# GLA mixer of a hybrid layer: 64-row TensorE tiles in place of zero padding, one output bank per head parity, and a later projection placed inside the pair loop

## The chip, the cores and the metric

One NeuronCore of a Trainium2 chip runs one program of two layers. The metric is the device time of one execution in microseconds (us). PE is TensorE, DVE VectorE, ACT ScalarE, POOL GpSimd, SP the queue that issues the weight loads. All arithmetic is fp32; a matmul in fp32 shows as two passes in the trace, so 16 records are 8 matmuls (a transpose is one pass).

## The reference

Two post-norm layers over 128 context tokens and 256 latent tokens. Each layer has three token mixers (gated DeltaNet, GLA, differential attention), a merge, an output projection and a grouped top-2 mixture of 16 experts. The change is in GLA and in the query projection of the attention that follows it. GLA, per head (4 heads, 64 key by 128 value dims, chunks of 64 tokens, forward and backward):

```
b = cumsum(glog)                    # within a chunk
a_intra = where(incl, (q*exp(b-b_ref)) @ (k*exp(b_ref-b)).T, 0)
q_dec, k_tail, g_tail = q*exp(b), k*exp(b_last-b), exp(b_last)
def step(S, xs):                    # over the chunks
    o = q_dec @ S + a_intra @ v
    S = S * g_tail[:, None] + k_tail.T @ v
```

The output is `o_forward + flip(o_backward)`, RMS-normed per head, times SiLU of a gate, and goes with the two other branches into the merge.

## The kernel before

One instruction stream is written out by hand for each engine; nothing is scheduled by a planner. The 384 tokens are three tiles of 128 (tile 0 the context, tiles 1 and 2 the latent grid). PSUM is used as seven banks in rotation: `take` on PE waits until the bank's last reader has freed it, `full` and `drained` are the waits of the other side. Weights come through a ring of three 2 MB slots, loaded by SP in the order in which PE's code first asks for them (`arrived`); a slot is loaded again when the product that used it has ended.

After DeltaNet a layer runs the dense products `gqk`, `gv`, `r` (24 matmuls of 128x512 each, line 395), then the GLA pair loop, then the product `dq` (the query projection of the attention), `finish_branch` for GLA, and the products `dk` and `dv`.

The pair loop (`PAIRS`, line 644) runs over three pairs p of (forward tile, backward tile): (0,0), (1,2), (2,1). In each pair:
- L650 and L657 form the decay sums on PE; ACT takes their exponentials (L1348 to L1355), DVE multiplies q and k into them (L1720), PE transposes the products (L666), ACT copies them out of PSUM (L1360, L1363, L1365).
- L675 makes the intra-chunk scores. Two heads share 128 key rows; so that a head sees only its own 64, the query operand `gl_qz` is kept twice, with the other head's half zero, and every matmul contracts over 128 rows. DVE masks the scores (L1726), one bank per direction d.
- L682 multiplies them with v; DVE moves the result into the output `ov` (L1734, L1730).
- Two steps, one per chunk. In each, for d = 0 and then d = 1, L702 multiplies the carried state into a bank of its own (DVE adds it to `ov`, L1742) and L712 forms the state's increment, which DVE adds to the decayed state (L1754, four instructions of 64x128). The state has the two heads of a pair side by side, 512 columns with zeros in the halves that belong to the other head.

When the three pairs are done, PE runs two short pieces for a modulation row (L442, L431), then `dq`, and only then waits for `branch_normed` and transposes the normed branch (L421). DVE reaches `branch_normed` after `finish` (L1532 to L1542). The lines of the loop around the wait:

```
                mod_columns(l, 10)
                mod_rows(l, 11)
                slot = arrived(pe, ("dq", l, 0))
                tokens_product("dq", l, lambda k: ring_in[slot][:, k, :])
                chunk_end["dq", l, 0] = ("dq", l, T - 1)
                finish_branch(l, 1)
```

Of the kernel before, what the change touches and what calls it, by code (L numbers as in the profile page):

```python
# [108 lines left out]
def program(nc, a, consts, y_prompt, y_sample, new_gdn, new_gla, new_k, new_v):  # L109
# [5 lines left out]
    with ExitStack() as ctx:  # L115
# [77 lines left out]
        dqv = late[:, 0:T * W5].rearrange("p (t w) -> p t w", t=T)  # L193
# [88 lines left out]
        def gl(name):  # L282

            return u_gla[:, GL[name] * W5:(GL[name] + 1) * W5]

        gl_qz, gl_k, gl_dec = u_gla[:, 3584:4608], u_gla[:, 4608:5120], u_gla[:, 5120:5632]
        gl_ln = u_gla[:, 5632:6144]

        def gla_at(d):
            return tail[:, d * W5:(d + 1) * W5]  # L290

        def gla_state(p, d):
            at = (min(p, 1) * DIR + d) * W5
            return s_gla[:, at:at + W5]
# [86 lines left out]
        def _(pe):  # L381
# [97 lines left out]
            for l in range(DEPTH):  # L479
# [163 lines left out]
                chunk_end["r", l, 0] = ("r", l, T - 1)  # L643
                for p, tiles in enumerate(PAIRS):
# [14 lines left out]
                    mm.then_inc(ready, 1)  # L659
                    for i, name in enumerate(("q_in", "k_in", "q_dec")):  # L660
# [7 lines left out]
                    for d, t in enumerate(tiles):  # L668
                        ps, ready = take(pe, ("gla_a", l, p, d))
                        if d == 0:  # L670
                            drained(pe, ("q_in", l, p))
                            drained(pe, ("k_in", l, p))
                        for h in range(H):
                            hp, par_ = h // 2, h % 2
                            mm = pe.matmul(ps[:, h * P:(h + 1) * P], gl_k[:, (d * 2 + hp) * P:(d * 2 + hp + 1) * P], gl_qz[:, par_ * W5 + (d * 2 + hp) * P:par_ * W5 + (d * 2 + hp + 1) * P],  # L675
                                           start=True, stop=True)
                        mm.then_inc(ready, 1)
                    for d, t in enumerate(tiles):
                        ps, ready = take(pe, ("gla_av", l, p, d))
                        drained(pe, ("gla_a", l, p, d))  # L680
                        for h in range(H):
                            mm = pe.matmul(ps[:, h * P:(h + 1) * P], gla_at(d)[:, h * P:(h + 1) * P],  # L682
                                           gvv[:, t, h * P:(h + 1) * P], start=True, stop=True)
                        mm.then_inc(ready, 1)
                    for step in range(2):
                        for d, t in enumerate(tiles):
                            ch = step if d == 0 else 1 - step
                            tok = slice(ch * HALF, (ch + 1) * HALF)
                            ps, ready = take(pe, ("gla_inter", l, p, d, step))
                            if step == 0 and d == 0:  # L690
                                drained(pe, ("q_dec", l, p))
                            if step == 1:
                                drained(pe, ("gla_ds", l, p, d, 0))
                            elif p == 1 and d == 0:
                                pe.wait_ge(sem("gla_state_in"), 64 * (l + 1))
                            elif p == 2:
                                drained(pe, ("gla_ds", l, 1, d, 1))
                            elif d == 0:
                                pe.wait_ge(sem("gla_zeroed"), l + 1)
                            for hp in range(2):  # L700
                                at = (d * 2 + hp) * P
                                mm = pe.matmul(ps[tok, hp * 256:(hp + 1) * 256], gl_dec[:, at + ch * HALF:at + (ch + 1) * HALF],  # L702
                                               gla_state(p, d)[:, hp * 256:(hp + 1) * 256], start=True, stop=True)
                            mm.then_inc(ready, 1)
                            if p == 2 and step == 1:
                                continue
                            ps, ready = take(pe, ("gla_ds", l, p, d, step))
                            if step == 0 and d == 0:
                                pe.wait_ge(sem("gla_decayed"), (l * 3 + p) * 4 + 4)
                            for hp in range(2):  # L710
                                at = (d * 2 + hp) * P
                                mm = pe.matmul(ps[:, hp * 256:(hp + 1) * 256], gl("k_tail")[tok, at:at + P],  # L712
                                               gvv[tok, t, hp * 256:(hp + 1) * 256], start=True, stop=True)
                            mm.then_inc(ready, 1)
# [339 lines left out]
        def _(pool):  # L1054
# [36 lines left out]
            for l in range(DEPTH):  # L1091
# [72 lines left out]
                for d in range(DIR):  # L1164
                    for hh in range(2):
                        if l:
                            full(pool, ("gla_inter", l - 1, 2, d, 1))
# [879 lines left out]
```

## Time and profile before

| what | value |
|---|---|
| median of 3 runs | 2439.39 us (2436.06 to 2440.36) |
| the profiled execution, first to last instruction | 2440.0 us |
| PE busy in it | 2189.8 us, 90% |
| DVE, ACT, POOL busy | 806.6, 448.7, 214.7 us |
| mean granted clock of PE | 0.966 of full speed |
| stretch from the first decay sum of GLA to the start of `dk`, layer 0 and layer 1 | 83.2 and 81.9 us |

The profiled execution's span is the only time that the page gives for it. A "busy" PE is one with a matmul in flight; a row of the timeline merges neighbouring instructions of one line, gives the start, the length to the end of the last one, their count, and in brackets the idle time before them with what ended it.

### The profile page before, as it was taken

How to read it: one execution, taken by the hardware profiler on the slowest of the kernel's cores; microseconds unless marked ns; L12 is line 12 of the kernel's file. 1: busy time of each engine (PE TensorE's matmuls, PEld its weight loads, DVE VectorE, ACT ScalarE, POOL GpSimd, SP SyncE). 2: the span in 40 equal slices, each digit the busy share in tenths (PEclk: the TensorE clock that was granted, in tenths of full speed). 3: DMA queues.
4: the chain of work that ended last, by engine and by line, in shares of the span. 5: the costliest groups of instructions: out<-in, count | busy, mean ns of one | idle time of the engine just before them, and what ended most of it. 6: DMA issues, size and time to landing. Idle time of an engine off the chain costs nothing.

```text
span 2440.0 us, 25315 instructions
## 1 busy us (share of the span) xinstructions
PE 2189.8 (90%) x9696; PEld 1211.5 (50%) x9696; DVE 806.6 (33%) x1602; ACT 448.7 (18%) x857; POOL 214.7 (9%) x221
## 2 busy tenths in 40 slices
PE   4998899998999879999699889999899978999994
PEld 1557774544444444344355777454444454344342
DVE  0526651625011421111552665162501250111115
ACT  0232114123100211011123111412300121111011
POOL 3024430000000000000002443000000000000000
PEclk9999999999999989999898999999999989999997
DMA  9321113144332359999722121313123228999993
GB/s 326 133 92 59 57 57 104 48 143 159 127 97 99 109 202 349 348 350 350 259 69 102 50 63 51 103 48 112 48 79 100 102 87 319 330 350 369 349 350 127
DMA packets 197474, 407.08 MB, mean 167 GB/s; under 512 B 6178, under 2 KB 6498, under 8 KB 197264
## 3 DMA queue, kind: packets, MB, share of 16 engines
q1 hardware_dynamic: 193136, 393.65, 45.9%
q0 software_dynamic: 4256, 12.28, 1.7%
q8 instruction: 57, 0.93, 0.2%
q14 instruction: 25, 0.20, 0.0%
HBM read 401.72 MB, written 4.19 MB: 166 GB/s over the span
## 4 chain that ended last, share of the span: by engine, by line
PE 72%; DMA 11%; DVE 10%; ACT 3%; issue 2%; SPq 1%; POOL 1%; DVEq 0%; POOLq 0%; ACTq 0%
PE bank L395 24%; DMA ring<-in_exp_w_up 10%; PE bank L545 6%; PE bank L885 6%; PE bank L913 6%; PE bank L873 5%; PE bank L497 5%; PE bank L805 5%; PE bank L923 2%; PE bank L431 1%; PE bank L581 1%; DMA ring<-in_w_mod 1%; PE bank L702 1%; PE bank L712 1%; PE bank L758 1%
## 5 line engine op out<-in xcount | busy, mean ns | idle before, releaser
L395 PE MATMUL bank<-ring,xt 128*128 128x512 f32 x1440 | 623.3, 593 | 8.5 <-ACT shared L1328 2.8
L395 PEld LDWEIGHTS bank<-ring,xt 128*128 128x128 f32 x1440 | 272.2, 190 | 354.2 <-issue 351.8
L885 PE MATMUL bank<-ring,shared 128*64 128x512 f32 x1280 | 295.5, 605 | 54.1 <-DMA ring<-in_exp_w_gate 29.9
L885 PEld LDWEIGHTS bank<-ring,shared 128*64 128x64 f32 x1280 | 88.1, 138 | 254.9 <-issue 167.6
L545 PE MATMUL bank<-shared 128*128 128x128 f32 x1408 | 184.2, 287 | 13.5 <-DVE shared L1678 5.5
L545 PEld LDWEIGHTS bank<-shared 128*128 128x128 f32 x1408 | 176.2, 201 | 15.8 <-issue 15.6
L1929 DVE TENSOR_TENSOR shared<-shared,bank 128x512 f32<-128x512 f32 x20 | 13.8, 688 | 444.6 <-PE bank L885 444.6
L913 PE MATMUL bank<-ring,shared 128*64 128x512 f32 x640 | 141.7, 595 | 1.2 <-issue 1.2
L873 PEld LDWEIGHTS bank<-qkvp,shared 128*128 128x128 f32 x1056 | 124.6, 198 | 20.2 <-issue 17.9
L873 PE MATMUL bank<-qkvp,shared 128*128 128x128 f32 x1056 | 128.8, 284 | 3.8 <-DVE qkvp L1916 3.8
L497 PE MATMUL bank<-xt,ring 128*128 128x384 f32 x384 | 124.3, 486 | 2.8 <-DVE xt L1525 2.8
L805 PE MATMUL bank<-ring,qkvp 128*128 128x512 f32 x288 | 124.7, 592 | 0.0
L1155 POOL TENSOR_TENSOR shared<-shared,cst 128x512 f32<-128x512 f32 x84 | 108.7, 1298 | 128.2 <-DVE shared L1631 63.6
L923 PE MATMUL bank<-shared 128*128 128x512 f32 x240 | 111.3, 601 | 1.5 <-ACT shared L1463 1.5
L497 PEld LDWEIGHTS bank<-xt,ring 128*128 128x128 f32 x384 | 72.8, 190 | 53.5 <-DVE xt L1525 3.2
L1936 DVE TENSOR_TENSOR shared<-shared,bank 128x512 f32<-128x512 f32 x108 | 70.9, 685 | 84.6 <-PE bank L923 84.6
L1446 ACT ACTIVATE shared<-bank 128x512 f32<-128x512 f32 x44 | 26.3, 597 | 344.7 <-PE bank L873 344.7
L805 PEld LDWEIGHTS bank<-ring,qkvp 128*128 128x128 f32 x288 | 54.6, 190 | 68.4 <-issue 68.4
L1833 DVE TENSOR_TENSOR shared<-shared,bank 128x512 f32<-128x512 f32 x24 | 16.5, 688 | 214.7 <-PE bank L805 214.7
L913 PEld LDWEIGHTS bank<-ring,shared 128*64 128x64 f32 x640 | 44.3, 137 | 84.5 <-issue 84.5
L431 PE MATMUL bank<-ring,scol 128*32 128x512 f32 x384 | 57.9, 729 | 26.8 <-DMA ring<-in_w_mod 24.9
L1424 ACT ACTIVATE shared<-bank 128x512 f32<-128x512 f32 x36 | 21.1, 597 | 271.7 <-PE bank L395 271.7
(342 smaller groups left out, 2119.1 us busy)
## 6 DMA issues: line engine op xcount, KB each, us to landing
ring<-in_exp_w_gate SPq DMA_DIRECT2D x80, 1024.0 KB, 7.9
ring<-in_exp_w_up SPq DMA_DIRECT2D x80, 1024.0 KB, 9.8
ring<-in_exp_w_down SPq DMA_DIRECT2D x80, 1024.0 KB, 10.7
ring<-in_w_in SPq DMA_DIRECT2D x32, 2048.0 KB, 9.5
ring<-in_w_mod SPq DMA_DIRECT2D x24, 2048.0 KB, 8.0
ring<-in_w_branch SPq DMA_DIRECT2D x6, 2048.0 KB, 7.7
ring<-in_w_out SPq DMA_DIRECT2D x4, 2048.0 KB, 7.7
shared<-in_ln_g POOLq DMA_DIRECT2D x4, 512.0 KB, 3.8
```

Source lines behind the costliest of these rows:

```text
L395: mm = pe.matmul(ps[:, 0:width], xtv[:, k, t * P:(t + 1) * P], w_of(k), start=(k == 0), stop=(k == KC - 1))
L431: mm = pe.matmul(ps[part:part + 32, :], scv[:, k, :], ring_in[slot][:, k, :], start=(k < 4), stop=(k >= 4))
L497: mm = pe.matmul(ps[:, 0:TOK], ring_in[slot][:, k, m % 4 * P:(m % 4 + 1) * P], xtv[:, k, :], start=(k == 0), stop=(k == KC - 1))
L545: mm = pe.matmul(ps[:, h * P:(h + 1) * P], lhs(h), rhs(h), start=True, stop=True)
L805: mm = pe.matmul(ps[:, :], ot[:, s * 4 + h, t * P:(t + 1) * P], ring_dn[slot][:, h, half * W5:(half + 1) * W5], start=(h == 0), stop=(h == ...
L873: mm = pe.matmul(banks[b][:, k * P:(k + 1) * P], htok[:, t, at:at + P], hot[:, t, :, :].rearrange("p u s -> p (u s)"), start=(t == 0), sto ...
L885: mm = pe.matmul(ps[u * SLOTS:(u + 1) * SLOTS, :], xg[:, at:at + SLOTS], w[:, u, k, :], start=(part == k == 0), stop=(part == 1 and k == 3))
L913: mm = pe.matmul(banks[EXPERT_BANKS["out"][half]][u * SLOTS:(u + 1) * SLOTS, :], ht[:, at:at + SLOTS], w[:, u, m, :], start=(m == 0), stop ...
L923: pe.matmul(banks[EXPERT_BANKS["back"][k]][:, :], hott[:, k // 2 * P:(k // 2 + 1) * P], oe[:, k % 2 * W5:(k % 2 + 1) * W5], start=True, st ...
L1155: pool.tensor_tensor(gd(d, "m").rearrange("p (h i) -> p h i", h=H), gd(d, "lt").rearrange("p (h i) -> p h i", h=H), fan(c(f"level{d}_{v}") ...
L1446: act.activation(xg[:, half * W5:(half + 1) * W5], ps[:, :], ACT.Copy).then_inc(free, 1)
L1936: dve.tensor_tensor(ycut, ycut, ps[:, :], ALU.add).then_inc(free, 1)
```

## The change

The padded operands go. `gl_qz` becomes `gl_q` (one copy, 512 columns), and each GLA state becomes 256 columns without zeros; the memsets of both are dropped. Every matmul on them now contracts over 64 rows and names the rows of its own head (`rows_`), so the two head parities `par_` stand in the upper and the lower 64 rows of the array. The scores of a pair go into two banks by parity, and no longer by direction. Products with v and with the carried state accumulate in the same two banks `gla_o`, which DVE reads once at the end of the pair. The first step of pair 0, whose state is zero, has no carried product, and DVE copies its increment instead of adding it. DVE's state update is two instructions of 128x128 for each step and direction. The product `dq` leaves its place behind the loop: token tile p is computed inside pair p, four matmuls before the transposes and four behind them, and ACT copies it out in the loop. Its result `dqv` moves to another buffer.

```diff
@@ PE, pair loop
+                dq_slot = arrived(pe, ("dq", l, 0))
+                def dq_part(t, part):
+                    if part == 0:
+                        take(pe, ("dq", l, t))
+                    b = fills["dq", l, t][0]
+                    for k in range(part * 4, part * 4 + 4):
+                        mm = pe.matmul(banks[b][:, :], xtv[:, k, t * P:(t + 1) * P], ring_in[dq_slot][:, k, :],
+                                       start=(k == 0), stop=(k == KC - 1))
+                    if part:
+                        mm.then_inc(bank_full[b], 1)
...
+                    dq_part(p, 0)
                     for i, name in enumerate(("q_in", "k_in", "q_dec")):
...
+                    dq_part(p, 1)
+                    pair = [take(pe, ("gla_a", l, p, par_)) for par_ in range(2)]
+                    drained(pe, ("q_in", l, p))
+                    drained(pe, ("k_in", l, p))
+                    for d in range(DIR):
+                        for hp in range(2):
+                            for par_, (ps, ready) in enumerate(pair):
+                                rows_ = slice(par_ * 64, par_ * 64 + 64)
+                                mm = pe.matmul(ps[:, gla_cut(d, hp)], gl_k[rows_, gla_cut(d, hp)], gl_q[rows_, gla_cut(d, hp)],
+                                               start=True, stop=True)
+                                if d == hp == 1:
+                                    mm.then_inc(ready, 1)
+                    out = [take(pe, ("gla_o", l, p, par_)) for par_ in range(2)]
+                    for par_, (ps, _) in enumerate(out):
+                        drained(pe, ("gla_a", l, p, par_))
+                        for d, t in enumerate(tiles):
+                            for hp in range(2):
+                                h = hp * 2 + par_
+                                pe.matmul(ps[:, gla_cut(d, hp)], gla_at(par_)[:, gla_cut(d, hp)], gvv[:, t, h * P:(h + 1) * P],
+                                          start=(d == hp == 0), stop=False, skip_group_check=True)
                     for step in range(2):
+                        if p == 0 and step == 0:
+                            drained(pe, ("q_dec", l, p))
+                        else:
+                            if step == 0:
                                 drained(pe, ("q_dec", l, p))
+                            for d in range(DIR):
+                                if step == 1:
+                                    drained(pe, ("gla_ds", l, p, d, 0))
...
+                            for hp in range(2):
+                                for d in range(DIR):
...
+                                    for par_, (ps, ready) in enumerate(out):
+                                        rows_ = slice(par_ * 64, par_ * 64 + 64)
+                                        mm = pe.matmul(ps[tok, gla_cut(d, hp)], gl_dec[rows_, at:at + HALF],
+                                                       gla_state(p, d)[rows_, hp * P:(hp + 1) * P],
+                                                       start=False, stop=(step == hp == d == 1), skip_group_check=True)
...
+                        pair = [take(pe, ("gla_ds", l, p, d, step)) for d in range(DIR)]
...
+                        for hp in range(2):
+                            for par_ in range(2):
+                                for d, t in enumerate(tiles):
...
+                                    mm = pe.matmul(pair[d][0][par_ * 64:par_ * 64 + 64, hp * P:(hp + 1) * P],
+                                                   gl("k_tail")[tok, at:at + 64], gvv[tok, t, h * P:(h + 1) * P],
+                                                   start=True, stop=True)
+                                    if hp == par_ == 1:
+                                        mm.then_inc(pair[d][1], 1)
...
                 mod_columns(l, 10)
                 mod_rows(l, 11)
-                slot = arrived(pe, ("dq", l, 0))
-                tokens_product("dq", l, lambda k: ring_in[slot][:, k, :])
-                chunk_end["dq", l, 0] = ("dq", l, T - 1)
                 finish_branch(l, 1)
@@ ACT, pair loop
-                    for hh in range(2):
-                        ins = act.activation(gl_qz[hh * 64:hh * 64 + 64, hh * W5:(hh + 1) * W5], ps[hh * 64:hh * 64 + 64, :], ACT.Copy)
-                    ins.then_inc(free, 1)
+                    act.activation(gl_q, ps[:, :], ACT.Copy).then_inc(free, 1)
...
+                    ps, free = full(act, ("dq", l, p))
+                    act.activation(dqv[:, p, :], ps[:, :], ACT.Copy).then_inc(free, 1)
@@ DVE, pair loop, after the masks
+                    for step in range(1 if p == 2 else 2):
...
+                            for hp in range(2):
+                                g0 = (d * 2 + hp) * 2 + ch
+                                ins = dve.scalar_tensor_tensor(out=s[:, hp * P:(hp + 1) * P], in0=s[:, hp * P:(hp + 1) * P],
+                                                               scalar=gla_gt(p)[:, g0:g0 + 1], in1=ps[:, hp * P:(hp + 1) * P],
+                                                               op0=ALU.mult, op1=ALU.add)
                             ins.then_inc(free, 1)
+                    for par_ in range(2):
+                        ps, free = full(dve, ("gla_o", l, p, par_))
...
+                            ins = dve.tensor_copy(o, new) if p == 1 else dve.tensor_tensor(o, o, new, ALU.add)
+                        ins.then_inc(free, 1)
```

Three places in the order of instructions show how this moves work. First PE, pair 1 (the pair in the middle) up to the next decay sum, before; a row counts matmuls and gives the output's partitions and columns:

```order
L657 MATMUL bank<-cst,shared 128x2 x4
L666 MATMUL bank<-cst,shared 128x128 x12
L675 MATMUL bank<-shared 128x128 x8
L682 MATMUL bank<-shared 128x128 x8
L702 MATMUL bank<-s_gla,shared 64x256 x2
L712 MATMUL bank<-shared 128x256 x2
L702 MATMUL bank<-s_gla,shared 64x256 x2
L712 MATMUL bank<-shared 128x256 x2
```

The last two rows come four times in all. The same place now (L660 is `dq_part`, L688 the transposes, L698 the scores, L708 the product with v, L730 the carried product, L746 the increment, L671 the next pair's decay sums):

```order
L678 MATMUL bank<-cst,shared 128x2 x4
L660 MATMUL bank<-ring,xt 128x512 x4
L688 MATMUL bank<-cst,shared 128x128 x12
L660 MATMUL bank<-ring,xt 128x512 x4
L698 MATMUL bank<-shared 128x128 x8
L708 MATMUL bank<-shared 128x128 x8
L730 MATMUL bank<-s_gla,shared 64x128 x8
L746 MATMUL bank<-shared 64x128 x8
L730 MATMUL bank<-s_gla,shared 64x128 x8
L746 MATMUL bank<-shared 64x128 x8
L671 MATMUL bank<-shared,cst 128x256 x6
```

The eight matmuls of `dq` stand around the transposes; both directions' carried products and increments of a step stand together, 8 matmuls of 128 columns where there were 4 of 256. Second, PE at the end of the loop, from the last carried product to `dk`, before:

```order
L702 MATMUL bank<-s_gla,shared 64x256 x4
L442 MATMUL bank<-cst,mrow 128x2 x4
L431 MATMUL bank<-ring,scol 32x512 x8
L395 MATMUL bank<-ring,xt 128x512 x24
L421 MATMUL bank<-cst,otok 128x128 x12
L442 MATMUL bank<-cst,mrow 128x2 x4
L395 MATMUL bank<-ring,xt 128x512 x48
```

And now:

```order
L730 MATMUL bank<-s_gla,shared 64x128 x8
L450 MATMUL bank<-cst,mrow 128x2 x4
L439 MATMUL bank<-ring,scol 32x512 x8
L429 MATMUL bank<-cst,otok 128x128 x12
L450 MATMUL bank<-cst,mrow 128x2 x4
L403 MATMUL bank<-ring,xt 128x512 x48
```

The 24 matmuls of `dq` no longer stand between the end of the loop and the transposes of the normed branch (L429, L421 before). Third, DVE in pair 1, from the masks to the next pair's products, before:

```order
L1726 COPY_PREDICATED shared<-cst,bank 128x512 x2
L1734 COPY otok<-bank 128x512 x2
L1742 TENSOR_TENSOR otok<-otok,bank 64x512
L1754 SCALAR_TENSOR_TENSOR s_gla<-s_gla,small,bank 64x128 x4
L1742 TENSOR_TENSOR otok<-otok,bank 64x512
L1754 SCALAR_TENSOR_TENSOR s_gla<-s_gla,small,bank 64x128 x4
```

The last two rows come four times in all. Now:

```order
L1761 COPY_PREDICATED shared<-cst,bank 128x512 x2
L1778 SCALAR_TENSOR_TENSOR s_gla<-s_gla,small,bank 128x128 x8
L1793 COPY otok<-bank 128x2x128 x4
L1755 TENSOR_TENSOR shared<-shared 128x256 x8
```

The state updates of both steps come first, and the two output banks are read behind the last of them.

## Rows read from the trace of the kernel before

**Rows 1.** The page's head: the span of the profiled execution.
```profile
span 2440.0 us, 25315 instructions
```

**Rows 2.** Timeline of PE in layer 0, GLA to `dk`: start, length, line, count, idle.
```profile
412.40 2.75 PE L650 MATMUL bank<-shared,cst 128*128 128x256 f32 x12
...
420.10 3.00 PE L675 MATMUL bank<-shared 128*128 128x128 f32 x16 [0.20 <-ACT shared L1363]
...
433.33 2.86 PE L650 MATMUL bank<-shared,cst 128*128 128x256 f32 x12
436.03 0.95 PE L657 MATMUL bank<-cst,shared 128*128 128x2 f32 x8
436.84 1.81 PE L666 MATMUL bank<-cst,shared 128*128 128x128 f32 x12
439.46 2.02 PE L675 MATMUL bank<-shared 128*128 128x128 f32 x16 [0.82 <-ACT shared L1363]
441.51 2.02 PE L682 MATMUL bank<-shared 128*128 128x128 f32 x16
443.47 1.08 PE L702 MATMUL bank<-s_gla,shared 128*64 128x256 f32 x4
444.47 1.13 PE L712 MATMUL bank<-shared 64*128 64x256 f32 x4
...
451.73 2.86 PE L650 MATMUL bank<-shared,cst 128*128 128x256 f32 x12
...
457.86 2.02 PE L675 MATMUL bank<-shared 128*128 128x128 f32 x16 [0.82 <-ACT shared L1363]
...
469.25 1.05 PE L442 MATMUL bank<-cst,mrow 128*128 128x2 f32 x8
...
472.09 20.87 PE L395 MATMUL bank<-ring,xt 128*128 128x512 f32 x48
492.79 1.47 PE L421 MATMUL bank<-cst,otok 128*128 128x128 f32 x12
494.10 0.95 PE L442 MATMUL bank<-cst,mrow 128*128 128x2 f32 x8
495.59 41.44 PE L395 MATMUL bank<-ring,xt 128*128 128x512 f32 x96 [0.54 <-ACT shared L1373]
```

**Rows 3.** Timeline of PE in layer 1, the ends of the same stretch.
```profile
1571.20 2.75 PE L650 MATMUL bank<-shared,cst 128*128 128x256 f32 x12
...
1653.05 41.44 PE L395 MATMUL bank<-ring,xt 128*128 128x512 f32 x96 [0.54 <-ACT shared L1373]
```

**Rows 4.** Timeline of DVE in layer 0, pair 1 and the end of GLA.
```profile
435.77 2.77 DVE L1720 TENSOR_TENSOR shared<-shared 128x256 f32<-128x256 f32 x8 [0.43 <-ACT shared L1349]
440.63 0.73 DVE L1726 COPY_PREDICATED shared<-cst,bank 128x512 f32<-128x512 uint32 x1 [2.09 <-PE bank L675]
...
445.74 1.43 DVE L1754 SCALAR_TENSOR_TENSOR s_gla<-s_gla,small,bank 64x128 f32<-64x128 f32 x4 [0.41 <-PE bank L712]
...
469.43 0.68 DVE L1742 TENSOR_TENSOR otok<-otok,bank 64x512 f32<-64x512 f32 x1 [0.58 <-PE bank L702]
470.14 1.76 DVE L1532 TENSOR_TENSOR shared<-otok 128x1536 f32<-128x1536 f32 x1
...
476.43 1.76 DVE L1542 TENSOR_TENSOR otok<-otok,shared 128x1536 f32<-128x1536 f32 x1
```

**Rows 5.** Timeline of PE, matmuls with 16 or 32 output rows, four column tiles in turn.
```profile
129.21 2.77 PE L454 MATMUL bank<-xt,wsmall 128*16 128x384 f32 x32
...
470.23 1.92 PE L431 MATMUL bank<-ring,scol 128*32 128x512 f32 x16
```

**Rows 6.** Timeline of PE in DeltaNet, after two waits.
```profile
245.65 1.08 PE L569 MATMUL bank<-cst,shared 128*128 128x128 f32 x4 [2.27 <-DVE shared L1635]
246.53 6.09 PE L545 MATMUL bank<-shared 128*128 128x128 f32 x32
```

**Rows 7.** Stretches: length, busy time of PE, PEld, DVE, ACT, POOL, granted clock, DMA.
```profile
245.00:250.00 5.00, 4.35 (x21) 4.38 (x22) 0.50 (x1) 1.19 (x2) 2.53 (x2) 0.50 0.92 319
280.00:285.00 5.00, 2.77 (x23) 2.44 (x22) 4.83 (x8) 0.00 (x0) 0.00 (x0) 1.00 0.00 0
```

More of the change, by code:

```diff
@@ L667, in _ @@
                         mm.then_inc(ready, 1)
[L668 to L684, printed above, removed]
-                    for step in range(2):
[L686 to L690, printed above, removed]
-                                drained(pe, ("q_dec", l, p))
-                            if step == 1:
-                                drained(pe, ("gla_ds", l, p, d, 0))
-                            elif p == 1 and d == 0:
+                    dq_part(p, 1)
@@ L704, in _ @@
[L704 to L713, printed above, removed]
@@ L1721, in _ @@
                         ins.then_inc(sem("gla_decayed"), 1)
-                    for d, t in enumerate(tiles):
-                        ps, free = full(dve, ("gla_a", l, p, d))
-                        if p == 0 and d == 0:
+                    for par_ in range(2):
+                        ps, free = full(dve, ("gla_a", l, p, par_))
+                        if p == par_ == 0:
                             dve.wait_ge(sem("gla_zeroed"), l + 1)
-                        dve.copy_predicated(h4(gla_at(d)), fan(c(f"sum{d}").bitcast(U32), H), h4(ps[:, :])).then_inc(free, 1)
@@ L1737, in _ @@
-                    for step in range(2):
+                        dve.copy_predicated(by_cut(gla_at(par_)), gla_mask, by_cut(ps[:, :])).then_inc(free, 1)
+                    for step in range(1 if p == 2 else 2):
+                        if step == 0:
+                            drained(dve, ("gla_gt", l, p))
                         for d, t in enumerate(tiles):
                             ch = step if d == 0 else 1 - step
-                            tok = slice(ch * HALF, (ch + 1) * HALF)
-                            ps, free = full(dve, ("gla_inter", l, p, d, step))
-                            dve.tensor_tensor(ov[tok, t, :], ov[tok, t, :], ps[tok, :], ALU.add).then_inc(free, 1)
-                            drained(dve, ("gla_inter", l, p, d, step))
-                            if p == 2 and step == 1:
-                                continue
-                            if step == 0:
-                                drained(dve, ("gla_gt", l, p))
@@ new lines, in _ @@
+                    for par_ in range(2):
+                        ps, free = full(dve, ("gla_o", l, p, par_))
+                        if p == par_ == 0:
+                            drained(dve, ("ot", l, 0, H - 1))
+                        if p == 2:
+                            drained(dve, ("gla_o", l, 1, par_))
+                        for d, t in enumerate(tiles):
+                            o, new = heads_of(ov[:, t, :], par_), ps[:, d * 256:(d + 1) * 256].rearrange("p (a e) -> p a e", a=2)
+                            if p == 0 and d == 0:
+                                link(dve.tensor_copy(o, new))
+                                continue
+                            ins = dve.tensor_copy(o, new) if p == 1 else dve.tensor_tensor(o, o, new, ALU.add)
+                        ins.then_inc(free, 1)
@@ L1758, in _ @@
+                for p in (0, 2):
+                    for par_ in range(2):
+                        drained(dve, ("gla_o", l, p, par_))
                 finish(l, 1)
```

83 lines of the change are left out of this document (43 added, 40 removed).

## Prediction

> **What bounds the kernel now.** I read the page first (a span of 2440.0 us, [rows 1]), then the timeline of PE through GLA in both layers, then DVE's and ACT's beside it, then stretches for the granted clock. In GLA PE is nearly always in work [rows 2]: the reader is to see that the start of each row is the end of the one before, and that the bracketed waits are short (0.20, 0.82 and 0.82 us). DVE runs in step with it: per step and direction it adds an output (about 0.7 us) and updates the state (1.43 us, [rows 4]), 2.1 us against PE's 1.00 for L702 and about as much for L712. Both engines are full, so work taken from PE alone would only wait for DVE; the change takes from both. The stretch that the change touches, from the first decay sum to the start of `dk`, takes 83.2 us in layer 0 [rows 2] and 81.85 in layer 1 [rows 3]. Everything behind it depends on it through PE's order, so what is won or lost here shifts the rest one for one. I make the sum for one layer, in three pieces.
>
> **Heads of the pairs (decay sums to scores).** Before, from L650 to L675: 7.70 us in pair 0 and 6.13 in pairs 1 and 2 [rows 2]. The work in it is 3.5 (433.33 to 436.84) and some 1.6 for twelve transposes (1.81 long, less the tail of the last), so 5.1; the rest is waiting for ACT and DVE. Now 3.45 us of `dq` (20.70 us between 472.09 and 492.79, in six) stand ahead of the transposes and 3.45 behind them, longer than any of those waits. They vanish: 2.6 + 1.0 + 1.0 = **4.6 us won**; `dq` itself costs the same in either place. ACT's extra copies of `dq` fall into its idle time, and its copy of q halves; if they did delay PE it would be by one copy of 0.6 us. The `dq` weights now take the ring slot that was the modulation row's, which is loaded when `gqk` ends, two products ahead of the loop, so no load is late.
>
> **Cores of the pairs (scores to the next decay sum).** Before: 13.23, 12.27 and 11.39 us [rows 2], 36.9 together. Now:
> - Scores: 8 matmuls, 16 passes, in two row tiles in turn. Full-size passes of 128 columns came 0.128 us apart (2.05 for 16). Two at a time gives 1.0. Both banks now fill at the end of the group, since parity is the innermost loop. So the mask, which ran under the other direction's scores before, is exposed: 0.15 (from the last issue of a bank to DVE's start at 440.63) + 0.73 + 0.15 (441.36 to PE's 441.51) = 1.03. Scores and wait: 2.05, as much as the 2.05 of before.
> - Product with v: the same 16 full-size passes, 2.05.
> - A group of carried products or of increments: 16 passes, four 64x64 tiles in turn. No row of before has row tiles side by side, so this is the unknown. Lower bound: a quarter of 2.05, 0.5. Upper bound: one after the other, 2.15 with the 0.10 that L702's four passes take above L650's (1.00 against 4 x 0.225). The nearest rows are the column tiles of [rows 5]: L431's 16 passes of 512 columns took 1.86 to the next issue, where a quarter of L395's 0.431 each would be 1.72. So four tiles do run side by side in fp32, at a surcharge of 0.13. I take 0.51 + 0.13 = 0.65.
> - Step 1 needs the state of both directions, and both increments end together: 0.15 + 4 x 0.36 + 0.15 = 1.74 us of wait [rows 4], in pair 0, where two copies stand in their place (0.35 each, as L1720's), 1.0. Before, one direction's update ran under the other's matmuls.
> - At the end of pairs 0 and 1, the next pair's second decay sum takes the bank of the first output, which DVE reads only behind the last updates: 0.15 + 1.44 + 0.7 + 0.15 = 2.44, less 0.9 for the first decay sum: 1.54 each.
>
> Pair 0: 2.05 + 2.05 + 0.65 + 1.0 + 1.3 = 7.05. Pair 1: 2.05 + 2.05 + 1.3 + 1.74 + 1.3 = 8.44. Pair 2 (no last increment): 7.79. With two waits of 1.54: 26.4, so **10.5 us won**.
>
> The page "TensorEngine Tiling (Array Packing)" of the Trainium skill, section "PSUM Bottleneck", says that tiling speeds up the array but not the emptying of PSUM, which may become the bound. The rows of DVE agree: of my 26.4 us 10.7 are waits for DVE. The same page's "Key Properties" has a change of tiling mode drain the array; L702's 0.10 is what that would be here, and by it the sum stays.
>
> **The end of the loop.** Before: 26.34 us from 469.25 to 495.59, of it 20.70 of `dq`: 5.64 net. `dq` covered DVE's `finish`. Now PE has only 2.84 us (469.25 to 472.09) before it waits for `branch_normed`, and `dk` is queued behind that wait. DVE starts 0.18 after the last issue (469.43), has four output additions of 256 columns (1.4), then 8.05 from 470.14 to the end of L1542 at 478.19 [rows 4], and PE answers 0.15 later: 9.8. Then transposes and columns, 2.80 less the 0.54 of a wait on ACT that `dq`'s copies caused: 2.26. So PE stands still for 7 us. In DeltaNet, after waits with little work between, the granted clock stood at 0.50, the lower level of 1.2 GHz [rows 7], and 32 passes took 6.09 us [rows 6] where two groups of L682's kind take 4.1: 2.0 lost. I add 2.0 (bounds 0 and 3). Together 14.1: **8.4 us lost**. A projection that hid this wait has been spent on waits half as long.
>
> **The sum.** 4.6 + 10.5 - 8.4 = 6.7 us in layer 0. Layer 1 was 1.3 us shorter before (its pair 0 has no slow stretch), so 5.4. Together 12.1: 2440.0 - 12.1 = 2427.9. The profiled span is 0.6 us above the median of the runs shown, 2439.39; I forecast **2428 us**. Changes under 0.2% (4.9 us) can't be told from none here: faster is below 2434.5, slower above 2444.3.
>
> **Rivals.**
> - *A floor under the passes (ends slower).* Small passes may not start closer than some interval, whatever the tiles. L454's 32 passes came 0.087 apart (2.77 in all, [rows 5]), L657's with two columns 0.1 [rows 2]. For the first, a quarter of a 384-column pass explains it, for the second the loading of 128 weight columns, so neither proves a floor. At 0.087 a group takes 1.5 and the scores 1.39: ten groups x 0.87 + 3 x 0.4 = 9.9 us more a layer, 2448 us. It decides for slower from about 0.08, and cancels the gain at about 0.07. At 0.06, halfway, a group takes 1.1: 4.5 more a layer, 2437, no change. The page "TensorE: Matmul & The Clock Gate", section "Wait — 56ns, not 53.3ns?", gives start-to-start floors of 25 ns or, with one decoding setting off, 62 ns a matmul; by the first my sum stays, by the second the time would be about the 2437 of this rival, and no row here tells which holds.
> - *Row tiles don't overlap.* Then groups take 2.15 and scores 2.05: 10 x 1.5 + 3 x 1.0 = 18 us a layer more, 2464 us. The column tiles speak against it; nothing in the trace has row tiles.
> - *The clock falls inside the loop.* Around each pair's end PE now works about half of 7 us. If it falls there twice a layer at 2.0 each: 2436, no change. Against it: PE was busy 2.77 of 5 us at 280 and the clock stayed at 1.00 [rows 7].
> - *More than forecast.* No clock loss at the end and groups of 0.5: 2421.
>
> **Chances.** Forecast, 2421 to 2434: 0.51. The halfway floor or the falling clock, 2435 to 2444: 0.27. A full floor or tiles in sequence, above 2444: 0.22. So faster 0.51, same 0.27, slower 0.22; the range 2420 to 2448 leaves out the sequence and the far end of the floor.
>
> **What will show it.** Right: groups L730 and L746 of 0.5 to 0.8 us for 16 passes; L708 starting about 2.05 after L698; no wait ahead of L688 or L698; PE idle some 7 us ahead of L429, and the matmuls behind it at the lower clock. The stretch from L671 to `dk` near 76.5 us in both layers. Wrong: groups of 1.1 or more, 2 us for the scores, a granted clock of 0.5 inside the pairs, or a short wait at L429.

## The result and the profile after

The changed kernel takes **2422.24 us** (median of 4 runs, 2419.19 to 2430.19) against 2439.88 of the kernel before on the same chip (median of 4 runs, 2436.06 to 2441.32): a ratio of 0.9933, with a 95% interval of 0.9913 to 0.9952. It is faster, by 16 us (0.0067 x 2440; 12 to 21 by the interval). The forecast was 2428 us, 12.1 us less than before; the time lies inside the range and near its fastest rival, 2421, though it got there by another road than that rival's (see the part on why).

The head of the page, to be read beside [rows 1]; the profiled run took 2424.14 us:

```profile
span 2422.3 us, 25499 instructions
```

The timeline of PE through GLA in layer 0 (start, length, line, tiles, shape, passes, idle time ahead of the row and what ended it), the answer to [rows 2]:

```profile
414.51 2.75 PE L671 MATMUL bank<-shared,cst 128*128 128x256 f32 x12
417.10 0.95 PE L678 MATMUL bank<-cst,shared 128*128 128x2 f32 x8
417.91 3.68 PE L660 MATMUL bank<-ring,xt 128*128 128x512 f32 x8
421.42 1.47 PE L688 MATMUL bank<-cst,shared 128*128 128x128 f32 x12
422.73 3.60 PE L660 MATMUL bank<-ring,xt 128*128 128x512 f32 x8
426.26 1.16 PE L698 MATMUL bank<-shared 64*128 64x128 f32 x16
...
431.97 0.67 PE L730 MATMUL bank<-s_gla,shared 64*64 64x128 f32 x16 [1.02 <-DVE s_gla L1770]
432.43 0.65 PE L746 MATMUL bank<-shared 64*64 64x128 f32 x16
433.00 1.13 PE L671 MATMUL bank<-shared,cst 128*128 128x256 f32 x4
435.11 1.99 PE L671 MATMUL bank<-shared,cst 128*128 128x256 f32 x8 [0.98 <-DVE otok L1793]
...
446.11 1.16 PE L698 MATMUL bank<-shared 64*128 64x128 f32 x16
448.17 2.02 PE L708 MATMUL bank<-shared 128*128 128x128 f32 x16 [0.90 <-DVE shared L1761]
450.13 0.67 PE L730 MATMUL bank<-s_gla,shared 64*64 64x128 f32 x16
450.61 0.62 PE L746 MATMUL bank<-shared 64*64 64x128 f32 x16
452.62 0.67 PE L730 MATMUL bank<-s_gla,shared 64*64 64x128 f32 x16 [1.39 <-DVE s_gla L1778]
453.08 0.65 PE L746 MATMUL bank<-shared 64*64 64x128 f32 x16
453.65 1.13 PE L671 MATMUL bank<-shared,cst 128*128 128x256 f32 x4
455.64 1.99 PE L671 MATMUL bank<-shared,cst 128*128 128x256 f32 x8 [0.85 <-DVE otok L1793]
...
473.73 1.05 PE L450 MATMUL bank<-cst,mrow 128*128 128x2 f32 x8
...
483.29 2.82 PE L429 MATMUL bank<-cst,otok 128*128 128x128 f32 x12 [6.65 <-DVE otok L1572]
485.90 1.71 PE L450 MATMUL bank<-cst,mrow 128*128 128x2 f32 x8
487.47 43.32 PE L403 MATMUL bank<-ring,xt 128*128 128x512 f32 x96
```

The reader is to see four things. In the heads no wait for the products or the transposes is left: from the last L671 to L698 each row starts where the one before it ends, with the two halves of `dq` (L660) around the transposes. In the core a group of 16 passes over the four 64x64 tiles takes 0.46 to 0.60 us from its start to the next work that waits for nothing. All waits of the core and of the decay sums behind it are for VectorE: the mask (0.90), the state (1.02 and 1.39), the output bank (0.98 and 0.85). And behind the loop PE stands still for 6.65 us, after which L429 takes 2.82 us where it took 1.47 before.

`dk` begins at 487.47. From the first decay sum that is 72.96 us, 10.2 less than before. Layer 1, the ends of the same stretch, the answer to [rows 3]:

```profile
1561.36 2.75 PE L671 MATMUL bank<-shared,cst 128*128 128x256 f32 x12
...
1630.15 2.82 PE L429 MATMUL bank<-cst,otok 128*128 128x128 f32 x12 [6.66 <-DVE otok L1572]
...
1634.33 43.33 PE L403 MATMUL bank<-ring,xt 128*128 128x512 f32 x96
```

72.97 us, 8.9 less. The last row gives something back: 96 passes of `dk` and `dv` in 43.33 us, 1.9 more than in [rows 3]. VectorE in pair 1 and at the end of layer 0, the answer to [rows 4]:

```profile
453.80 1.12 DVE L1778 SCALAR_TENSOR_TENSOR s_gla<-s_gla,small,bank 128x128 f32<-128x128 f32 x4 [1.32 <-PE bank L746]
454.83 1.41 DVE L1793 COPY otok<-bank 128x256 f32<-128x256 f32 x4
...
481.47 1.76 DVE L1572 TENSOR_TENSOR otok<-otok,shared 128x1536 f32<-128x1536 f32 x1
```

Stretches of layer 0 around the end of the loop (length, busy time of PE, PEld, DVE, ACT and POOL, granted clock, DMA share, GB/s), to be read like [rows 7]:

```profile
463.00:468.00 5.00, 4.80 (x27) 2.41 (x25) 0.17 (x1) 1.60 (x4) 0.00 (x0) 1.00 0.04 9
...
476.60:483.20 6.60, 0.04 (x4) 0.00 (x0) 6.18 (x7) 2.09 (x3) 0.00 (x0) 0.83 0.81 285
483.20:487.40 4.20, 4.11 (x20) 4.12 (x21) 2.98 (x9) 1.96 (x4) 2.03 (x3) 0.50 0.51 181
487.40:490.00 2.60, 2.60 (x4) 1.22 (x5) 0.00 (x0) 0.00 (x0) 0.00 (x0) 0.50 0.00 0
```

The clock is granted in full inside the loop, falls while PE stands still, and stays at the lower level, 1.2 GHz, through L429, L450 and into `dk`.

The account: 10.2 + 8.9 = 19.1 us won between the first decay sum and `dk`, less 1.9 a layer at the start of `dk`, leaves 15.3, close to the 16 us of the runs. The spans differ by 17.7; what lies between is other work: from `dk` in layer 0 to the first narrow product of layer 1 (L454, now L462) all nine traces below and these two range from 781.6 to 789.4 us, without order.

### The profile page after: what moved, and what is told of

It is laid out like the page before. It is cut to its first block, busy times and chain, and to the rows that moved or that the text cites. A ratio compares the mean times of both kernels' runs of the same rounds, so it can differ in the third digit from the quotient of the medians.

```text
span 2422.3 us, 25499 instructions
## 1 busy us (share of the span) xinstructions
PE 2157.9 (89%) x9840; PEld 1194.9 (49%) x9840; DVE 772.7 (32%) x1546; ACT 446.5 (18%) x851; POOL 210.4 (9%) x217
## 4 chain that ended last, share of the span: by engine, by line
PE 72%; DMA 11%; DVE 10%; issue 2%; ACT 2%; POOL 1%; SPq 1%; DVEq 0%; POOLq 0%; ACTq 0%
PE bank L403 23%; DMA ring<-in_exp_w_up 9%; PE bank L553 7%; PE bank L919 6%; PE bank L947 6%; PE bank L907 5%; PE bank L505 5%; PE bank L839 5%; PE bank L957 2%; DMA ring<-in_w_mod 2%; PE bank L660 2%; PE bank L589 1%; PE bank L439 1%; PE bank L792 1%; DMA ring<-in_exp_w_gate 1%
## 5 line engine op out<-in xcount | busy, mean ns | idle before, releaser
L403 PE MATMUL bank<-ring,xt 128*128 128x512 f32 x1344 | 588.6, 599 | 7.5 <-ACT shared L1360 2.8
L403 PEld LDWEIGHTS bank<-ring,xt 128*128 128x128 f32 x1344 | 256.8, 192 | 333.5 <-issue 331.1
L553 PE MATMUL bank<-shared 128*128 128x128 f32 x1408 | 185.4, 288 | 13.7 <-DVE shared L1708 5.7
L439 PE MATMUL bank<-ring,scol 128*32 128x512 f32 x384 | 57.5, 726 | 29.9 <-DMA ring<-in_w_mod 28.0
```

The costliest lines, as they stand in the source:

```text
L403: mm = pe.matmul(ps[:, 0:width], xtv[:, k, t * P:(t + 1) * P], w_of(k), start=(k == 0), stop=(k == KC - 1))
L439: mm = pe.matmul(ps[part:part + 32, :], scv[:, k, :], ring_in[slot][:, k, :], start=(k < 4), stop=(k >= 4))
L553: mm = pe.matmul(ps[:, h * P:(h + 1) * P], lhs(h), rhs(h), start=True, stop=True)
```

## The experiments

The question was how the two halves of the change (the tiles, the moved `dq`) share in the 16 us, whether the tiles are fast for the reason given, and whether the waits seen are what they cost. My theory: the tiles win some 25 us, and `dq` inside the pairs loses part of it through the wait at L429 and the clock. The rival: `dq` inside is a gain of its own.

**dq back behind the loop** (in PE's program; ACT's copies follow):

```diff
-                    dq_part(p, 0)
...
-                    dq_part(p, 1)
...
                 mod_rows(l, 11)
+                slot = arrived(pe, ("dq", l, 0))
+                tokens_product("dq", l, lambda k: ring_in[slot][:, k, :])
...
                 finish_branch(l, 1)
```

> The changed kernel with all three dq tiles back behind the loop, ahead of the branch's finish. Theory (the move of dq lost more than it won): the 6.65 us that PE stood still ahead of L429 in each layer vanishes, since 20.7 us of dq cover it; the matmuls behind it are back at the lengths of before (12 passes of L429 in 1.47 us, not 2.82), which gives back some 4 us a layer; the heads of the three pairs lose their cover and get 4.6 us longer together. 4.6 - 6.65 - 4.0 = -6.0 us a layer, -12 in all: about 2410 us. Rival 1 (the granted clock falls because of the waits inside the pairs, not of the one behind the loop): the slow matmuls stay, -2 us a layer, 2418. Rival 2 (dq inside the pairs won as much as it lost): heads 8 us or more longer a layer, 2422 or more.

Measured: 2412.12 us (5 runs; before 2439.17, 17 runs), ratio 0.990 (0.9883 to 0.9917). That is 24 us less than before and, by the ratios, 8 less than the changed kernel; the two intervals just touch. PE in layer 0:

```profile
435.50 1.16 PE L683 MATMUL bank<-shared 64*128 64x128 f32 x16 [0.39 <-ACT shared L1378]
...
457.59 3.61 PE L439 MATMUL bank<-ring,scol 128*32 128x512 f32 x16
...
481.83 1.47 PE L429 MATMUL bank<-cst,otok 128*128 128x128 f32 x12
...
484.63 41.44 PE L403 MATMUL bank<-ring,xt 128*128 128x512 f32 x96 [0.54 <-ACT qkvp L1388]
```

The wait at L429 is gone, L429, L450 and `dk` run at the lengths of before again, as the theory had it. Rival 2 falls, and rival 1 for these rows. The heads got longer by less than the 4.6 us expected: the tile in pair 0 was worth 2.6 in layer 0 (7.43 us from L658 to L683, part of it at a low clock, against 11.75 less 6.9 of `dq`) and 2.3 in layer 1, those in pairs 1 and 2 only 0.44 each: in the compact loop the wait ahead of the scores is 0.39 us without any cover, where it was 0.82 in [rows 2]. Against that L439 took 3.61 us in layer 0, at a granted clock of 0.56 and then 0.50, and 1.92 in layer 1; whether waits inside the pairs brought that on, as rival 1 has it, is open.

**Only the third tile behind the loop:**

```diff
-                    dq_part(p, 0)
+                    if p < 2:
+                        dq_part(p, 0)
...
                 mod_rows(l, 11)
+                dq_part(2, 0)
+                dq_part(2, 1)
...
                 finish_branch(l, 1)
```

and likewise for `dq_part(p, 1)` and for ACT's copy of the third tile.

> The changed kernel with only the third dq tile moved behind the loop, ahead of the branch's finish. Theory: 3.45 of the 6.65 us wait ahead of L429 are filled, and pair 2 gets back its own waits in the head, 1.0 us: -2.4 us a layer if the matmuls behind the remaining 3.2 us stay slow (L429 at 2.8 us), 2417 in all; -6 a layer if the granted clock holds through a wait of 3 us (L429 at 1.5 us), 2410. Rival (the wait is set by the end of DVE's work, and that moves with the head of pair 2 as a whole): the loop ends 2.5 us earlier and the wait is 3.2 us too, which gives the same time by another road; the row of L429 and the length of pair 2's head (12.98 us now) tell the two apart. No gain at all, 2422, would say that the third tile was worth in the loop what it costs behind it.

Measured: 2406.57 us (4 runs), ratio 0.9861 (0.9844 to 0.9877). The expectation counted one half of a tile (3.45 us) as the whole of it; a tile is 6.9 us, and so it covers the whole of the 6.65 us wait:

```profile
468.72 3.31 PE L439 MATMUL bank<-ring,scol 128*32 128x512 f32 x16
471.96 7.39 PE L660 MATMUL bank<-ring,xt 128*128 128x512 f32 x16
479.19 1.47 PE L429 MATMUL bank<-cst,otok 128*128 128x128 f32 x12
```

L429 follows without a wait and at full clock. From the first decay sum to `dk` it is 66.32 us in layer 0 and 64.67 in layer 1, 6.6 and 8.3 less than in the changed kernel (layer 0 lost 1.4 of it at L439, 3.31 us where layer 1 took 1.92), and `dk` and `dv` take 41.45 us again. So the third tile was misplaced: in pair 2 it bought 0.44 us, behind the loop it buys 6.65 and the clock.

**dq inside the pairs alone** (the kernel before with the same moves of `dq` and its result's place, and nothing else):

> The kernel before with only the move of dq into the pairs' heads (and the place of its result that this needs); the loop's padded matmuls stay as they were. Theory (the two parts add up): heads 4.6 us shorter a layer, the end 8.4 us longer by idle PE and a slow clock at L421, and some 2 us more for slow matmuls at the start of dk: 5 to 6 us a layer, 2450 us, slower than before. Then the tiles alone bring the 20 to 30 us that the two together don't show. Rival (dq inside is a gain by itself, since the end's wait is hidden in part by DVE's shorter work): 2440 or less.

Measured: 2443.56 us (12 runs), ratio 1.0021 (1.0008 to 1.0034): slower, by 5 us (2 to 8), half of what was expected. PE at the end of the loop:

```profile
485.74 1.05 PE L442 MATMUL bank<-cst,mrow 128*128 128x2 f32 x8
...
494.74 2.82 PE L421 MATMUL bank<-cst,otok 128*128 128x128 f32 x12 [6.09 <-DVE otok L1557]
...
498.92 43.56 PE L395 MATMUL bank<-ring,xt 128*128 128x512 f32 x96
```

The wait and the slow clock are there without any tile. The heads won 5.5 us (4.76 + 4.87 + 4.87 beside `dq`, against 19.96 in [rows 2]), the end lost 7.5 (13.18 against 5.64), where 4.6 and 8.4 were expected; in layer 0 pair 0's core ran at full clock and won 1.0 more, and only one of the two layers began `dk` slowly. With the tiles alone at -24 and `dq` alone at +5, the sum is -19, and the two together measure -16: nearly additive. The rival falls.

**Tiles in sequence:**

```diff
-                            for hp in range(2):
+                            for par_, (ps, ready) in enumerate(out):
                                 for d in range(DIR):
...
-                                    for par_, (ps, ready) in enumerate(out):
+                                    for hp in range(2):
```

and likewise for the increments: each tile's two matmuls (four passes) come one behind the other.

> The changed kernel with the carried products and increments in another order: all matmuls of one 64x64 tile one after the other, then those of the next tile. The same instructions, banks and waits. Theory (the four tiles run side by side only where neighbours in the queue belong to different tiles): a group of 16 passes, 0.46 to 0.57 us now, takes between 1.0 (two of four neighbours overlap) and 1.7 us (four passes of 0.128 in each tile before the next begins); ten groups a layer make 5 to 12 us a layer, 2432 to 2446 us. Rival (a small pass costs its issue alone, whatever tile it is in, or the order in the queue doesn't matter): groups stay at 0.5 to 0.6, 2422.

Measured: 2425.13 us (5 runs), ratio 0.9946 (0.9932 to 0.996), on the changed kernel's own to within the intervals. A group is still issued in about half a microsecond (0.48 to 0.62 from its start to the next work without a wait):

```profile
451.85 0.69 PE L730 MATMUL bank<-s_gla,shared 64*64 64x128 f32 x16
452.33 0.68 PE L746 MATMUL bank<-shared 64*64 64x128 f32 x16
```

So my theory of the order fell: neighbours in the queue need not be of different tiles. Either each tile takes passes in ahead, or small passes are cheap by themselves; the next run tells the two apart.

**All products of a group in one tile** (the carried products alone; the kernel so leaves half of the state and half of the output rows out of them):

```diff
-                                        rows_ = slice(par_ * 64, par_ * 64 + 64)
-                                        mm = pe.matmul(ps[tok, gla_cut(d, hp)], gl_dec[rows_, at:at + HALF],
+                                        rows_ = slice(0, 64)
+                                        mm = pe.matmul(ps[0:HALF, gla_cut(d, hp)], gl_dec[rows_, at:at + HALF],
```

> The changed kernel with all 8 matmuls of a carried product (L730) in one and the same 64x64 tile: rows 0 to 63 of the operands, output rows 0 to 63, the same columns and banks; the state rows 64 to 127 and the other output rows are so left out of the product. Theory (the four tiles run side by side, each with its own short queue, so that the order in the queue does not matter but the tile does): 16 passes of 128 columns one after the other, 0.107 to 0.128 us each as in the full-size groups, 1.7 to 2.05 us a group where it is 0.48 now; five groups a layer, 6 to 8 us a layer, 2434 to 2438 us. Rival (a pass with 64 rows and 64 columns of weights is cheap by itself, in whatever tile): 0.5 us a group as now, 2422.

Measured: 2438.06 us (10 runs; before 2440.16, 15 runs), ratio 0.9996 (0.9982 to 1.001): the whole gain is gone. PE in pair 0:

```profile
431.46 1.60 PE L730 MATMUL bank<-s_gla,shared 64*64 64x128 f32 x13 [1.02 <-DVE s_gla L1770]
432.80 0.32 PE L746 MATMUL bank<-shared 64*64 64x128 f32 x1
432.91 0.27 PE L730 MATMUL bank<-s_gla,shared 64*64 64x128 f32 x1
...
433.01 0.27 PE L730 MATMUL bank<-s_gla,shared 64*64 64x128 f32 x1
433.02 0.33 PE L746 MATMUL bank<-shared 64*64 64x128 f32 x3
433.12 0.27 PE L730 MATMUL bank<-s_gla,shared 64*64 64x128 f32 x1
433.18 0.65 PE L746 MATMUL bank<-shared 64*64 64x128 f32 x11
433.76 1.13 PE L671 MATMUL bank<-shared,cst 128*128 128x256 f32 x4
```

From the first pass (431.46) to the fourteenth (432.91) it is 1.45 us, 0.11 a pass, where all 16 took 0.46 in the changed kernel. The increments behind them in the program (L746, whose first pass here is in another tile) start at 432.80, while three passes of L730 are still to start. So the tiles do run side by side, and each pass takes nearly what a full-size one does (1.96 us for the 16 of L708, 0.12 each) in its own tile. Not all of the lost time is the passes': five groups, each 1.27 us longer than now, make 12.7 us in two layers, and the clock fell in this loop too, to 0.50 at the last group of layer 0 (16 passes in 3.58 us from 477.73), with no wait there longer than 1.41 us.

**Outputs first:** VectorE reads both output banks ahead of the second state update; `outputs` holds the lines that read them.

```diff
-                    for step in range(1 if p == 2 else 2):
+                    for step in range(2):
+                        if step == 1:
+                            outputs(p, tiles)
+                            if p == 2:
+                                continue
```

> The changed kernel with VectorE reading both output banks of a pair ahead of the second state update, not behind it. Theory (the next pair's second decay sum waits for a bank that DVE reads late, and that wait is on the path): the idle 0.98 and 0.85 us ahead of L671 in pairs 1 and 2 go to near nothing, and in pair 2 nothing changes: -1.8 us a layer, -3.7 in all, 2418 to 2419 us. Rival (the state of the next pair is then late, or the wait comes back at the transposes): the same time as now, 2422.

Measured: 2417.75 us (5 runs), ratio 0.9905 (0.9888 to 0.9923), by the ratios 7 us less than the changed kernel; the intervals overlap, so what the order is worth is read from the trace. The decay sums of pairs 1 and 2 now run through as one row of 12 passes, 2.86 us long, with no wait inside, and the stretch to `dk` is 70.27 and 70.01 us, 2.7 and 3.0 less: 2.4 of it in the decay sums of pairs 1 and 2 (2.69 us each from L671 to L678, where it was 3.94 and 3.82), 1.83 of that the two waits. The rest lies in the L450 behind L429, where the clock came back earlier (1.39 and 1.13 us, not 1.71), and `dk` and `dv` are back at 41.45 us, 1.9 less a layer. The wait at L429 stays at 6.65, so why the clock came back earlier is not shown; the decay sums alone are 4.8 us in two layers, where 3.7 were expected.

**Third tile behind and outputs first together:**

> The third dq tile behind the loop (as in the run on that, 2406.6 us) and the outputs ahead of the second state update together. Theory (the two touch different waits): 2406.6 - 3.7 = 2403 us. Rival (a shorter loop only moves VectorE's work into the end): 2406 to 2407.

Measured: **2397.23 us** (5 runs), ratio 0.9821 (0.9804 to 0.9839). The gains add up within the interval: from 0.9933 the third tile took 0.0072 and the order of VectorE 0.0028, which makes 0.9833. Both of these hold the fast start of `dk`, which can be won only once; the stretch up to `dk` is 2.2 and 2.4 us shorter than with the third tile behind alone, so the full sum is somewhat more than the trace explains. It is the fastest version of the study beside the two below, and 25 us under the changed kernel.

**Scores by parity**, on top of that:

```diff
-                    for d in range(DIR):
-                        for hp in range(2):
-                            for par_, (ps, ready) in enumerate(pair):
+                    for par_, (ps, ready) in enumerate(pair):
+                        for d in range(DIR):
+                            for hp in range(2):
```

> The same as the run with the third tile behind and the outputs first, with one more edit: the scores (L698) run parity by parity, the four matmuls of one bank ahead of the four of the other. Theory (the 0.90 us that PE waits for the first mask ahead of the product with v begin when the first bank is full, and the order of passes does not cost the overlap, as the run with the tiles in sequence showed): the first bank is full some 0.5 us earlier, and the wait falls from 0.90 to 0.4: three waits a layer, -1.5 us a layer, -3 in all: 2400 us. Rival 1 (row tiles one after the other don't overlap: scores take 2 us, not 1.1): +0.5 a pair, 2406. Rival 2 (the second mask is then what the product waits for): the same as without the edit, 2403.

Measured: 2396.76 us (5 runs), ratio 0.9827 (0.9804 to 0.9851): the same as without it. PE in pair 1:

```profile
444.94 1.71 PE L700 MATMUL bank<-shared 64*128 64x128 f32 x16
447.01 2.02 PE L710 MATMUL bank<-shared 128*128 128x128 f32 x16 [0.36 <-DVE shared L1783]
```

The wait fell to 0.36, as expected, but the scores grew from 1.16 to 1.71, and from the first score to the product it is 2.07 us as before. The single starts in the traces show why: in either order the eighth pass of the first bank starts 0.88 us after its first, 0.11 apart, so the first bank is full no earlier. The other row tile's first pass starts 0.55 us late here, when three of the eight are still to start, and 0.01 us late when the two tiles take turns.

**The second tile in the waits of pair 1's core:** its halves between scores and product, and between the first increments and the second carried product.

> The run with the third tile behind and the outputs first, with the two halves of the second dq tile moved from pair 1's head into the two waits of its core: one between the scores and the product with v, one between the first increments and the second carried product. Theory (in the head of pair 1 this tile covers only some 0.2 to 0.4 us, as pair 2's head without one shows; the core's waits of 0.90 and 1.39 us are there to be filled): -1.9 us a layer, -3.8 in all, 2393 to 2394 us. Rival (the waits come back, behind the half or in pair 2, since VectorE's chain from pair 1 to pair 2 sets the pace): 2397 or more.

Measured: 2399.11 us (5 runs; before 2445.74 on this chip, 9 runs), ratio 0.9815 (0.9802 to 0.9829). PE in pair 1:

```profile
439.32 3.70 PE L660 MATMUL bank<-ring,xt 128*128 128x512 f32 x8
442.86 1.95 PE L712 MATMUL bank<-shared 128*128 128x128 f32 x16
...
445.77 3.70 PE L660 MATMUL bank<-ring,xt 128*128 128x512 f32 x8
449.40 0.67 PE L734 MATMUL bank<-s_gla,shared 64*64 64x128 f32 x16
```

Both waits are gone, and pair 1 is 1.8 to 1.9 us shorter (17.62 from L671 to L671, against 19.54 and 19.40 in the run with the third tile behind and the outputs first). In the time this is not resolved: the two ratios' intervals overlap. In the trace layer 1 keeps the gain (60.51 us up to `dk`, 62.30 in that run), while layer 0 loses most of it to the clock (63.78 and 64.09): L439 took 3.64 us and the third tile behind it 8.34, where layer 1 took 1.92 and 7.13.

## Why the prediction was right, and where it was off

- **Heads: right.** 4.6 us a layer forecast; 19.96 before, 4.85 + 5.23 + 5.23 now beside `dq` and the waits for the output bank, so 4.65. (The prediction calls the waits of before short and names three; 1.53 us ahead of the transposes of pair 0 and 1.14 ahead of pair 2's last carried product stand beside them, and its sums hold both.) In the compact loop alone the same cover was worth 3.2 to 3.5 (pair 0's 2.3 to 2.6 and twice 0.44), because the loop shortened those waits too.
- **Cores: right in kind, too small.** Forecast 26.4 us with the two waits for the output bank, measured 6.74 + 7.54 + 7.10 + 0.98 + 0.85 = 23.2: 13.7 won in layer 0, not 10.5. The terms that were mis-sized: a group of 16 passes 0.46 to 0.60 us, not 0.65 (the lower bound, a quarter of 2.05, was the answer: 0.46 to 0.49 ahead of another group, and 0.1 more ahead of full-size matmuls); the state update 1.12 for four on 128x128, not 1.44 from four on 64x128 of [rows 4], so the wait 1.39, not 1.74; the wait for the output bank 0.98 and 0.85, not 1.54. Scores with their mask are 2.07 (2.05), the product 1.96 (2.05). That both engines' work had to shrink for this is argued from the rows of before; no run takes from PE alone.
- **End of the loop: right.** 13.74 us against 14.1, with 6.65 of idle PE forecast as 7. The clock's 2.0 up to `dk` came out as 1.9 (4.18 us from L429 to `dk`, where 2.26 were net of the wait before). That size is luck: it was what 32 passes lost in DeltaNet, and here 12 transposes and 8 short passes lost it. What the forecast left out is that the clock stays down into `dk`: 1.9 more a layer. The bounds, 0 to 3, should have reached to 4.
- **The sum.** 6.7 and 5.4 forecast, 10.2 and 8.9 measured up to `dk`, 8.3 and 7.0 with its slow start. The fault is the core's three terms, 3.2 a layer, and the slow start of `dk` hides 1.9 of it. So the time is nearer to the forecast than its terms are, and nearer still to the rival of 2421 by luck: that one had no clock loss, and here it is 3.8 a layer. The runs say more than these two traces: 16 us, against 12.1 forecast and 15.3 in the account.
- **Rivals.** The floor under the passes falls: 0.46 over 16 passes is 0.03 us each. The page "TensorE: Matmul & The Clock Gate" of the Trainium skill, section "Wait — 56ns, not 53.3ns?", gives two floors between starts, 25 and 62 ns a matmul. For passes in different tiles the trace bears out neither, and the measurement decides: their mean distance is 29 ns, under the 62, and in the run in one tile two of them start 0.01 us apart (433.01 and 433.02), under the 25. Row tiles do overlap: 16 passes of the scores take 1.16 us, not 2.05. Tiles in sequence fall too: the run in one tile shows what they would have cost, 1.3 us for each of the five groups that it put in sequence (2.30 us from L730 to L671 in pair 0, where the changed kernel has 1.03). The falling clock inside the loop did not come in the changed kernel: it was granted 1.00 from 414.51 to 473.70. It did come in the run in one tile.

The page "TensorEngine Tiling (Array Packing)" of the Trainium skill, section "PSUM Bottleneck", says that tiling does not speed up the emptying of PSUM, which may become the bound. The trace agrees in part: of the 7.54 us of pair 1's core 2.3 are waits for VectorE's work on PSUM, and filling these two with `dq` took 1.8 off the pair; the rest of the core is PE's own.

## What to carry to other kernels

Cover is worth what the wait that it fills costs, and moving a filler leaves the wait that it used to fill: here the tiles alone take 24 us, the moved `dq` hands back a third, and one of its three tiles left behind the loop gets that back and more. Order VectorE's queue by who waits: reading the banks that PE needs next, ahead of a state that it needs later, cost nothing here. After a change that removes padding, look for waits anew, since the old ones moved.

## What the runs showed of the hardware

- Four 64x64 fp32 tiles run fully side by side: 16 passes in 0.46 to 0.60 us in turn and 0.48 to 0.62 with four passes of a tile in a row, against 0.11 each in one tile. Eight in a row on one row tile did lose overlap (1.71 us for 1.16).
- Passes behind a busy tile in the program started ahead of passes that still waited for it (432.80 against 432.91 in the run in one tile). In that run and in the scores by parity, passes in a free tile began when three passes for the busy one were still to start; with four in a row, one running and three waiting, they began 0.01 us later. From these three runs it looks as if a tile takes three waiting passes ahead, and a fourth holds up the others; no run tests that by itself.
- In all five kernels that have a `dq` tile behind the loop the granted clock fell just behind pair 2 in one layer, with PE at work (1.00 up to 457.5 us in the first, then 0.56 and 0.50): L439 took 2.85 to 3.64 us there, and 1.92 in the other layer of the same trace. What picks the layer is open.
- After the same wait ahead of L429, 6.65 us, the clock stayed down into `dk` in the changed kernel (43.3 us for 96 passes) and was back by then in the run with the outputs first (41.45). What decides it is open.
- One of VectorE's state updates took 0.34 us for 128x128 and 0.35 for 64x128: twice the elements in the same time. Four in a row took 1.12 and 1.43 us; why the larger ones also follow closer is open.
